# Second attention: divided probabilities and values, three passes in place of one full-width product

## What is computed

```python
def chunk_band_mixer(h, w_in, q_g, k_g, rel_table):
    q, k, v = jnp.split(h @ w_in, 3, axis=-1)          # 16 heads of 64
    q = rmsnorm(q, q_g); k = rmsnorm(k, k_g)
    # each 64-frame chunk attends to itself and the 8 chunks before it
    logits = einsum('bhqd,bkhd->bhqk', q_c, k_c) * scale + bias
    p = softmax(logits)
    o = einsum('bhqk,bkhd->bqhd', p, v_c)
```

## Time and profile before

| | us |
|---|---|
| median of 3 runs | 2912.32 (2911.82 to 2914.94) |
| the profiled execution, its own time | 2912.41 |
| its span (first to last instruction) | 2910.6 |
| TensorE busy | 2762.1 (95% of the span) |
| VectorE busy | 1486.0 (51%) |
| ScalarE busy | 1136.6 (39%) |
| GpSimd busy | 827.6 (28%) |

### The profile page before, as it was taken

How to read it: one execution, slowest core, us unless ns; L and a number is a source line. 1 busy time by engine, 2 the same in 40 slices (tenths; PEclk the granted TensorE clock), 3 DMA queues, 4 the chain that set the end, 5 groups by cost and what they waited for, 6 DMA issues and landing times. The chain is left out here.

```text
span 2910.6 us, 38781 instructions
## 1 busy us (share of the span) xinstructions
PE 2762.1 (95%) x14678; PEld 2375.5 (82%) x14678; DVE 1486.0 (51%) x2412; ACT 1136.6 (39%) x2489; POOL 827.6 (28%) x468
## 2 busy tenths in 40 slices
PE   7797798999899999999989999999989999999999
PEld 6697687888788888888879998888878888888887
DVE  5899566651544444444441115777335444444444
ACT  5578465551322222222244546666322222222221
POOL 2121423202332322322335442111033322333232
PEclk9899799999999999999989999999999999999999
DMA  4110000011111111111021110001011111111111
GB/s 168 44 44 1 26 9 5 17 51 44 66 51 51 43 50 43 46 54 43 29 112 44 47 41 6 24 10 69 16 65 51 44 57 43 43 58 46 47 46 63
DMA packets 38755, 132.43 MB, mean 46 GB/s; under 512 B 4240, under 2 KB 12608, under 8 KB 36960
## 3 DMA queue, kind: packets, MB, share of 16 engines
q1 hardware_dynamic: 38624, 130.68, 13.1%
HBM read 122.22 MB, written 13.69 MB: 47 GB/s over the span
## 5 line engine op out<-in xcount | busy, mean ns | idle before, releaser
L330 PE MATMUL banks<-XH,WH 128*128 128x512 f32 x1408 | 439.9, 394 | 5.3 <-POOL WL L291 4.3
L291 POOL TENSOR_TENSOR WL<-WR,WH 128x1024 fp32r<-128x1024 f32 x132 | 333.1, 2531 | 380.7 <-ACT WH L245 380.7
L330 PE MATMUL banks<-XL,WH 128*128 128x512 f32 x1408 | 440.3, 394 | 0.0
L330 PE MATMUL banks<-XH,WL 128*128 128x512 f32 x1408 | 436.4, 391 | 0.0
L260 ACT ACTIVATE Y<-U,CONVB,CONVW 128x1024 f32<-128x1024 f32 x88 | 109.5, 1245 | 643.1 <-DVE U L386 643.1
L386 DVE TENSOR_TENSOR U<-banks,RB 128x1024 f32<-128x1024 f32 x88 | 107.7, 1224 | 415.6 <-PE banks L330 406.3
L330 PEld LDWEIGHTS banks<-XH,WH 128*128 128x128 f32 x1408 | 265.5, 189 | 63.1 <-POOL WL L291 4.5
L330 PEld LDWEIGHTS banks<-XH,WL 128*128 128x128 f32 x1408 | 265.2, 188 | 60.9
L330 PEld LDWEIGHTS banks<-XL,WH 128*128 128x128 f32 x1408 | 265.7, 189 | 58.0
L376 DVE TENSOR_TENSOR XT<-XT,banks 128x1024 f32<-128x1024 f32 x176 | 214.4, 1218 | 164.7 <-PE banks L346 164.7
L299 POOL TENSOR_TENSOR AL<-Y,AH 128x1024 fp32r<-128x1024 f32 x44 | 106.3, 2416 | 615.1 <-ACT AH L268 615.1
(11 more groups left out here) (226 smaller groups left out, 5412.7 us busy)
## 6 DMA issues: line engine op xcount, KB each, us to landing
WR<-in_ffn SPq DMA_DIRECT2D x132, 512.0 KB, 3.5
QWR<-in_qkv SPq DMA_DIRECT2D x12, 1536.0 KB, 6.5
XT<-in_xT SPq DMA_DIRECT2D x16, 512.0 KB, 7.5
OWR<-in_w_o SPq DMA_DIRECT2D x16, 512.0 KB, 3.2
spill<-XT SPq DMA_DIRECT2D x8, 512.0 KB, 14.0
XT<-spill SPq DMA_DIRECT2D x8, 512.0 KB, 8.4
outT<-XT SPq DMA_DIRECT2D x8, 512.0 KB, 2.6
near<-strip SPq DMA_DIRECT2D x1, 3072.0 KB, 20.9
```

The lines of the kernel that those rows point to most:

```text
L291: pool.tensor_tensor(WL[:, ch % RING, :], WR[:, ch % RING, :], WH[:, ch % RING, :].bitcast(F32), ALU.subtract).then_inc(w_lo, 1)
L330: mm = pe.matmul(u[:, h * HALF:(h + 1) * HALF], w[:, ch % RING, db * P:(db + 1) * P], x[:, db, h * HALF:(h + 1) * HALF], start=(db == 0 an ...
```

## The change

`values` becomes three F32R products a block: high probabilities by high values, high by low, low by high. ScalarE writes the high part `PTH` of every bank, VectorE the low part `PTL` (bank minus `PTH`) of every bank, behind ScalarE. The values' high parts are made by GpSimd (`values(t)`: a rounding copy and a subtraction for each of the 64 tiles); for the first three head pairs they lie in slabs that are free until outputs reach them, for the later ones in a new buffer of two head pairs. The low parts overwrite the value columns of the tile. TensorE's `turn(g)` now waits for the low part of the unit before, bank by bank, and `values` for both parts and for GpSimd.

```diff
-        assert 4 * 4 * D <= low_tiles * TILE
+        assert 4 * 4 * D + 2 * 4 * TT * P <= low_tiles * TILE
+        late_vh = nc.alloc_sbuf_tensor_at("VH1", [P, 2, TT, P], F32R, offset=m.at + 4 * 4 * D)
...
-        PT = u.take("PT1", [P, 2, PW], F32)
+        PTH = u.take("PTH1", [P, 2, PW], F32R)
+        PTL = u.take("PTL1", [P, 2, PW], F32R)
...
+        early_vh = [x[:, d, :].rearrange("p (t n) -> p t n", n=P) for x, d in ((c.MH, 7), (c.ML, 7), (c.MH, 6))]
+
+        def value_high(t):
+
+            k, i = divmod(t, TT)
+            return early_vh[k][:, i, :] if k < len(early_vh) else late_vh[:, k % 2, i, :]
+
+        def value_low(t):
+
+            return lows[region(t)][:, t - edges[region(t)], NH * HD:PROJ]
+
...
+        def parts_before(g):
+
+            return g + seconds_before(g)
+
+        def parts(g):
+
+            n, first = blocks(place(g)[1]) * P, cut(blocks(place(g)[1])) * P
+            return [(0, 0, first)] + ([(1, first, n)] if first < n else [])
...
             for g in range(ALL):
-                k, i, h = place(g)
-                n = blocks(i) * P
-                pt = PT[:, g % 2, :]
-                if n <= 3 * P:
-                    act.wait_ge(t_first, g + 1)
-                    act.activation(pt[:, 0:n], TP[0][:, 0:n], ACT.Copy).then_inc(pt_act, 1)
-                else:
-                    c0 = cut(blocks(i)) * P
-                    act.wait_ge(t_second, seconds_before(g + 1))
-                    act.activation(pt[:, c0:n], TP[1][:, 0:n - c0], ACT.Copy).then_inc(pt_act, 1)
+                k = place(g)[0]
+                for bank, a, b in parts(g):
+                    if bank == 0:
+                        act.wait_ge(t_first, g + 1)
+                    else:
+                        act.wait_ge(t_second, seconds_before(g + 1))
+                    act.activation(PTH[:, g % 2, a:b], TP[bank][:, 0:b - a], ACT.Copy).then_inc(pt_hi, 1)
...
+            def values(t):
+                raw = tile(t)[:, NH * HD:PROJ]
+                if t >= 2 * TT:
+                    pool.wait_ge(pv_ready, (t // TT - 1) * UNITS)
+                pool.tensor_copy(value_high(t), raw).then_inc(v_hi, 1)
+                pool.wait_ge(v_hi, t + 1)
+                pool.tensor_tensor(value_low(t), raw, value_high(t).bitcast(F32), ALU.subtract).then_inc(v_ready, 1)
+
...
+            pool.wait_ge(pj_ready, TILES)
+            for i in range(TT):
+                values(i)
             for k in range(1, GROUPS):
...
                 for i in range(TT):
-                    doubled(k * TT + i)
+                    t = k * TT + i
+                    doubled(t)
+                    if t >= TT + 2:
+                        values(t - 2)
+            for t in range(TILES - 2, TILES):
+                values(t)
...
             def turn(g):
                 k, i, h = place(g)
                 pe.wait_ge(exp_done, g + 1)
-                if acts_before(g):
-                    pe.wait_ge(pt_act, acts_before(g))
-                if firsts_before(g):
-                    pe.wait_ge(pt_dve, firsts_before(g))
+                if g >= 1:
+                    pe.wait_ge(pt_lo, parts_before(g - 1) + 1)
                 n = blocks(i)
                 for b in range(n):
                     bank, seat = divmod(b, cut(n))
+                    if b == cut(n):
+                        pe.wait_ge(pt_lo, parts_before(g))
...
             def values(g):
                 k, i, h = place(g)
                 if h == 0 and g >= 2:
                     pe.wait_ge(mo_ready, g // 2)
-                pe.wait_ge(pt_act, acts_before(g + 1))
-                if firsts_before(g + 1):
-                    pe.wait_ge(pt_dve, firsts_before(g + 1))
+                pe.wait_ge(v_ready, k * TT + i + 1)
+                pe.wait_ge(pt_lo, parts_before(g + 1))
                 last = blocks(i) - 1
+                cols = slice(h * HD, (h + 1) * HD)
                 for b in range(last + 1):
-                    mm = pe.matmul(OP[:, h * HD:(h + 1) * HD], PT[:, g % 2, b * P:(b + 1) * P],
-                                   tile(k * TT + i - last + b)[:, (NH + h) * HD:(NH + h + 1) * HD],
-                                   start=(b == 0), stop=(b == last))
+                    t = k * TT + i - last + b
+                    hi, lo = (x[:, g % 2, b * P:(b + 1) * P] for x in (PTH, PTL))
+                    pe.matmul(OP[:, cols], hi, value_high(t)[:, cols], start=(b == 0), stop=False)
+                    pe.matmul(OP[:, cols], hi, value_low(t)[:, cols], start=False, stop=False)
+                    mm = pe.matmul(OP[:, cols], lo, value_high(t)[:, cols], start=False, stop=(b == last))
...
             for g in range(ALL):
                 k, i, h = place(g)
-                if blocks(i) >= 4:
-                    dve.wait_ge(t_first, g + 1)
-                    c0 = cut(blocks(i)) * P
-                    dve.tensor_copy(PT[:, g % 2, 0:c0], TP[0][:, 0:c0]).then_inc(pt_dve, 1)
+                for bank, a, b in parts(g):
+                    dve.wait_ge(pt_hi, parts_before(g) + bank + 1)
+                    dve.tensor_tensor(PTL[:, g % 2, a:b], TP[bank][:, 0:b - a], PTH[:, g % 2, a:b].bitcast(F32),
+                                      ALU.subtract).then_inc(pt_lo, 1)
```

More of the change, by code:

```diff
@@ L538, in band_phase @@
         s_ready, max_done, exp_done = sem("s_ready"), sem("max_done"), sem("exp_done")
-        t_first, t_second, pt_act, pt_dve = sem("t_first"), sem("t_second"), sem("pt_act"), sem("pt_dve")
+        t_first, t_second, pt_hi, pt_lo = sem("t_first"), sem("t_second"), sem("pt_hi"), sem("pt_lo")
+        v_hi, v_ready = sem("v_hi"), sem("v_ready")
         pv_ready, rcp_done, mo_ready = sem("pv_ready"), sem("rcp_done"), sem("mo_ready")
@@ L592, in cut @@
             return n if n < 4 else (n + 1) // 2
-        def firsts_before(g):
-            return sum(blocks(place(v)[1]) >= 4 for v in range(g))
+        def parts_before(g):
[3 more added lines that the diff above has]
+            return [(0, 0, first)] + ([(1, first, n)] if first < n else [])
         @block.sync
@@ L827, in turn @@
                     mm.then_inc(t_second, 1)
-            def acts_before(g):
-                return g
             def values(g):
```

## The result

The changed kernel takes 3033.0 us in the median of 4 runs (2997.5 to 3052.1), the kernel before 2913.3 beside it. The ratio is 1.032, with a 95% interval of 1.027 to 1.038; it leaves out the runs that were over 1.5% above the fastest; the two medians, with them, give 3033.0 / 2913.3 = 1.041. The spread of 55 us, where the kernel before has 3 in the same comparison, belongs to the result, as will be seen. The forecast was 2958, range 2944 to 2974: the direction is right, the size is not, 120 us by the medians (94 by the ratio of 1.032) in place of 46.

The account below looks back on a forecast made before the run. TensorE was taken to bound the kernel, with a few us of waits a head pair. Loop +40.9 and opening +4.5 made 45.4 us on the profiled 2912.4: 2958 us, range 2944 to 2974.

Parts of the forecast that it names:

- the first one of the working: Fourth head pair of the attention loop: TensorE is the bound, 34.50 of 37.91 us at the full granted clock.
- the opening: Loop's start: TensorE's first heads waits 4 us for GpSimd, low clock lasts 0.5 us longer; together +4.5 us.
- The price of a product: Values on TensorE: loads 0.112 us apart set the pace, a block goes from 0.224 to 0.336 us; bill 53.8 us.
- The rival of a load at the matmul's pace: Values: F32R products of 64 columns 0.06 us apart instead of 0.112; 2912 us, not slower; chance 0.04.
- the dropped second load: Values: second load of the same stationary operand dropped, two loads a block as before; 2922 us; chance 0.04.
- nothing is hidden: Odd iterations: low part comes late, waits stay, the whole 53.8 us shows; +58 with the opening, 2971 us; chance 0.20.
- waits swallow more: Odd iterations keep their length wherever work allows; a head pair +3.7 us instead of +4.8, total 2950 us; chance 0.12.
- The chain's new end: Odd iterations: VectorE's subtraction in every unit adds 0.14, 0.27, 0.40 us; one-block ones become 2.42 from 2.28.
- GpSimd: Ahead of the loop: eight value tiles at 0.75 us each, 6.0 us, make TensorE's first heads 4 us late.
- The rule of the Trainium skill: Values' loads on TensorE: several times faster with 128 weights and non-FP32 type; would make the bill a gain.

Follow-up runs that it names:

- the wide products: The changed kernel with each product moving both heads' 128 value columns instead of 64, the other head's half unused; 2965.4 us, ratio 1.017. Also called the wide kernel.
- the copies exchanged: The kernel before, with ScalarE copying every unit's first bank and VectorE the second, awaited only ahead of the second bank's transposes; 2903.5 us, ratio 0.9962.
- the F32 experiment: The changed kernel with all divisions and waits, but one full-width F32 product a block, of the high copies alone; 2929.1 us, ratio 1.0056.
- mended: The changed kernel with 128 moving columns, and GpSimd making the loop's first two doubled rows before the eight divided tiles; 2957.3 us, ratio 1.0144.
- with the opening mended: The changed kernel with 64 moving columns, and GpSimd making the loop's first two doubled rows before the eight divided tiles; 3031.2 us.

## Why the prediction was wrong

**The step that failed** is the first one of the working, and it was not noticed as a step: "In the fourth head pair ... at the full granted clock". I priced each block at 0.112 us a load and never asked whether the engine would be granted that clock for other work. The clock came up in the prediction only at the opening, as "a stall there keeps it low a little longer, 0.5 us", that is as a matter of stalls. The runs show in its place: at the low clock a load of `values` costs 0.21 us, not 0.112, and 85.6 us of the profiled loop (427.7 less 342.1, the wide products) and 3 of the output projection are clock (68 us by the medians), with no stall ahead of the fall; as many instructions with 128 moving columns do not lose it. None of my rivals was this one.

**The price of a product** was right. At full clock five-block iterations are 2.98 us odd (forecast 3.01) and 3.31 even (1947.73 to 1951.04, forecast 3.34), a head pair 42.6 (42.7), the stage + 47.0 with wide products (45.4). The rival of a load at the matmul's pace is excluded by that, and so is the dropped second load; "nothing is hidden" too, which wanted + 58, and "waits swallow more", which wanted a head pair of 41.6. By the medians the wide kernel is 51 us slower than the one before (2965.4 and 2914.4), 4 more than its stage; its profiled loop began 9.4 us later (1790.3 for 1780.9) in code that the change does not touch, the other runs' 1.4 earlier to 6.5 later, and that stays open.

**The chain's new end** was right in kind: one-block odd iterations 2.40 against 2.42, and the copies exchanged gained the 10 us that the chain promised. Taken alone, with the opening, it costs 14.4 us of stage in place of 10 (the F32 experiment against the kernel before): 6.4 in the first head pair, where I had 5.3, 6.1 in the six middle ones for 4.8, and 1.8 in the last, which I had at nothing there. In the first the low clock lasts 8 us longer; for the last no run separates the causes.

**GpSimd** was right: 0.77 us a tile for 0.75, 4.34 us of wait for 4; mended, it gave 4.7 back.

**The rule of the Trainium skill** that I weighed, fast loads for a type other than FP32 ("TensorE: Matmul & The Clock Gate", section "Weight-path perf modes"), stayed out of play: at full clock the narrow F32R loads start 0.11 us apart, as the F32 ones did. Of the clock the Trainium skill, "TensorE: Matmul & The Clock Gate", section "Why this matters for your kernels", says to leave no idle gaps between bursts of matmuls. Here that would have warned of nothing: 0.03 us of 27.30 were idle ahead of the fall.

What stays open is why the spells last as they do, and why the loop keeps the low clock from 2144.9 on; the runs show that narrow short units hold it, not by how little it is missed. The spread of the changed kernel's times (55 us) fits a clock that falls a varying number of times: the mean clocks of its four executions are 0.960, 0.954, 0.941 and 0.939 for 2997.5, 3016.6, 3049.5 and 3052.1 us, and the loop stages are 427.7 at 0.72 and, with the opening mended, 394.6 at 0.79. Why it varies was not tested.

## What to carry to other kernels

When a change replaces wide or full-width matmuls by narrower or rounded ones, ask what the engine's clock will be as well as how far apart the instructions start: a window before the change shows the clock that the old work was granted, not what the new work will get. If the loads set the pace, moving more columns than needed can be free, as 128 for 64 was here, and may pay for itself. And when an odd wait is found, look whose queue the awaited instruction stands in: exchanging two copies between engines gave 0.4% where the division of operands cost 3%.

## What the runs showed of the hardware

- The granted clock fell from 2.4 to 1.2 GHz with TensorE busy 27.27 of the 27.30 us before, and did so in one head pair after another, 51.1 us apart; the same program with 128 instead of 64 moving columns kept 2.4 GHz in its middle head pairs.
- With as many loads and matmuls and the same waits, two rounded products of 64 columns had a mean clock of 0.91 over the loop and one full-width F32 product of 64 columns 0.98; two rounded ones of 128 columns had 0.97, and 1.00 after the opening.
- Loads of 128 columns, each with a product of 64, start 0.11 us apart at 2.4 GHz and 0.21 at 1.2 GHz.
- 128 moving columns take no more time than 64 where each product has its own load: the same iteration of five blocks at full clock is 2.68 us with either.
